# Three score products and neighbouring value products of the sample group written to different partition groups of PSUM

## The reference, cut to what matters

```
s_c = einsum('bqgrd,bcgd->bgrqc', qg, kc) + tab[...]        # 63 compressed keys
...
s_s = einsum('bqgrd,bgqksd->bgrqks', qg, k_sel) + tab[...]  # up to 16 blocks of 64 keys
...
s_w = einsum('bqgrd,bkgd->bgrqk', qg, kvw[:, :, 0]) + tab[...]   # 513 window keys
...
o_x = einsum(p_x, v_x)          # p_x = masked softmax(s_x), for each of the three branches
```

## Time and profile before

| | |
|---|---|
| median of 3 runs | 1839.0 us (1838.51 to 1839.18) |
| the profiled execution | 1834.96 us, span 1833.4 us, mean TensorE clock 0.907 of full |
| TensorE matmul busy | 1605.6 us, 88% |
| VectorE busy | 759.3 us, 41% |
| ScalarE busy | 504.2 us, 28% |
| GpSimd busy | 108.2 us, 6% |
| sample group | about 1400 to 1750 us of the span |

### The profile page before, as it was taken

How to read it: one execution, slowest core, us unless ns; L and a number is a source line. 1 busy time by engine, 2 the same in 40 slices (tenths; PEclk the granted TensorE clock), 3 DMA queues, 4 the chain that set the end, 5 groups by cost and what they waited for, 6 DMA issues and landing times. The chain is left out here.

```text
span 1833.4 us, 22894 instructions
## 1 busy us (share of the span) xinstructions
PE 1605.6 (88%) x8053; PEld 1234.2 (67%) x8053; DVE 759.3 (41%) x1821; ACT 504.2 (28%) x919; POOL 108.2 (6%) x147
## 2 busy tenths in 40 slices
PE   6989999998987998989999999996675888888686
PEld 3877787777765786878768767765353655566375
DVE  3057776776676102001541460451652333344313
ACT  3133233323331100021331332332441233333102
POOL 0011112111210000000010001001000000000000
PEclk7989999999997997998997997996786999999888
DMA  5075435543460340242052015004005544442111
GB/s 174 3 208 164 141 93 164 161 143 92 135 192 26 105 124 1 70 104 69 1 117 57 24 44 130 23 0 133 6 1 160 143 134 120 116 116 70 47 56 47
DMA packets 141544, 170.20 MB, mean 93 GB/s; under 512 B 46532, under 2 KB 108348, under 8 KB 141132
## 3 DMA queue, kind: packets, MB, share of 16 engines
q1 hardware_dynamic: 130120, 129.38, 24.4%
q0 software_dynamic: 11344, 39.79, 7.9%
HBM read 149.20 MB, written 24.32 MB: 95 GB/s over the span
## 5 line engine op out<-in xcount | busy, mean ns | idle before, releaser
L273 PE MATMUL psum<-arena 128*128 128x260 f32 x1536 | 356.2, 390 | 7.4 <-DMA arena<-in_ssd_w_in 7.4
L1484 PE MATMUL psum<-arena 128*128 128x260 f32 x1408 | 335.3, 396 | 7.8 <-DMA arena<-in_nsa_w_in 5.4
L273 PEld LDWEIGHTS psum<-arena 128*128 128x128 f32 x1536 | 291.8, 192 | 60.4 <-DMA arena<-in_ssd_w_in 7.8
L1484 PEld LDWEIGHTS psum<-arena 128*128 128x128 f32 x1408 | 271.2, 196 | 64.4 <-issue 12.5
L326 PE MATMUL psum<-arena 128*128 128x128 f32 (+9 forms) x1367 | 198.2, 289 | 96.5 <-DVE arena L1763 24.0
L326 PEld LDWEIGHTS psum<-arena 128*128 128x128 f32 (+9 forms) x1367 | 154.3, 148 | 148.3 <-issue 57.9
L1053 PE MATMUL psum<-arena 128*128 128x260 f32 x656 | 149.4, 390 | 8.8 <-PEq L593 6.9
L1053 PEld LDWEIGHTS psum<-arena 128*128 128x128 f32 x656 | 127.0, 194 | 31.0 <-issue 9.6
L1190 PE MATMUL psum<-arena 128*128 128x252 f32 x512 | 123.8, 404 | 5.4 <-ACT arena L1185 5.4
L1190 PEld LDWEIGHTS psum<-arena 128*128 128x128 f32 x512 | 103.7, 205 | 22.3 <-issue 4.8
L1688 ACT ACTIVATE arena<-arena 128x128 f32<-128x128 f32 (+3 forms) x128 | 71.9, 562 | 131.6 <-DVE arena L1780 126.8
(11 more groups left out here) (261 smaller groups left out, 1740.1 us busy)
## 6 DMA issues: line engine op xcount, KB each, us to landing
arena<-in_cache_kv SPq DMA_DIRECT2D x128, 256.0 KB, 4.1
arena<-in_ssd_w_in SPq DMA_DIRECT2D x16, 1024.0 KB, 5.4
arena<-in_nsa_w_in SPq DMA_DIRECT2D x16, 1024.0 KB, 5.2
arena<-scr_rows POOLq DMA_DIRECT2D x16, 520.0 KB
arena<-in_ssd_w_in SPq DMA_DIRECT2D x16, 512.0 KB
arena<-scr_rows POOLq DMA_DIRECT2D x8, 1024.0 KB, 6.5
arena<-in_state_ssm POOLq DMA_DIRECT2D x16, 512.0 KB, 6.9
out_ssm_sample<-arena POOLq DMA_DIRECT2D x16, 512.0 KB, 7.0
```

The lines of the kernel that those rows point to most:

```text
L273: mm = nc.tensor.matmul(psum[:, b + h, 0:HALF], w[:, k, n % 2 * P:(n % 2 + 1) * P], xn[:, k, h * HALF:(h + 1) * HALF], start=(k == 0), sto ...
L1484: mm = nc.tensor.matmul(psum[:, pair + h, 0:HALF], w[:, k, at * P:(at + 1) * P], xn[:, k, h * HALF:(h + 1) * HALF], start=(k == 0), stop=( ...
```

## The change

Three places. On TensorE the scores of the two key halves and of the window (now all on L1951, g outside, the three key sets inside) go to PSUM partitions 0, 32 and 64; the value products of neighbouring key tiles go in turn to partitions 0 and 32 (`out(r, n % 2)`), the compressed branch's product moves behind the eight selected ones. On VectorE the bias addition of the selected scores is split by halves, since they lie in different partitions, and the two halves of the selected and of the window output are added while they are taken out of PSUM: two copies and two additions instead of two copies, with one more wait of VectorE for itself.

```
-                for a in range(2):
-                    for g in range(2):
-                        nc.tensor.matmul(psum[0:NH, a, :], qcur[:, g, :], kselt[:, g, a, :], start=(g == 0), stop=(g == 1))
+                keys = (lambda g: kselt[:, g, 0, :], lambda g: kselt[:, g, 1, :],
+                        lambda g: kwint[:, g].rearrange("p a n -> p (a n)"))
                 for g in range(2):
-                    nc.tensor.matmul(psum[0:NH, 2, :], qcur[:, g, :], kwint[:, g].rearrange("p a n -> p (a n)"),
-                                     start=(g == 0), stop=(g == 1))
+                    for a in range(3):
+                        nc.tensor.matmul(psum[32 * a:32 * a + NH, a, :], qcur[:, g, :], keys[a](g),
+                                         start=(g == 0), stop=(g == 1))
...
-                def out(r):
-                    return psum[0:NH, 2, r * 256:(r + 1) * 256] if r < 2 else psum[0:NH, 0, 0:256]
+                def out(r, e):
+                    return psum[32 * e:32 * e + NH, 2, r * 256:(r + 1) * 256] if r < 2 else psum[32 * e:32 * e + NH, 0, 0:256]
...
-                nc.tensor.matmul(out(0), pcT[0:NCS, NH:2 * NH], vcmp[0:NCS, :], start=True, stop=True)
                 for n in range(8):
-                    nc.tensor.matmul(out(1), ptb[:, n * NH:(n + 1) * NH], pages_s[j][:, n % 4, n // 4, 256:512],
-                                     start=(n == 0), stop=False)
-                nc.tensor.matmul(out(1), ptn[:, 0:NH], vnew[j][:, 0:256], start=False, stop=True)
+                    nc.tensor.matmul(out(1, n % 2), ptb[:, n * NH:(n + 1) * NH], pages_s[j][:, n % 4, n // 4, 256:512],
+                                     start=(n < 2), stop=(n == 6))
+                nc.tensor.matmul(out(0, 0), pcT[0:NCS, NH:2 * NH], vcmp[0:NCS, :], start=True, stop=True)
+                nc.tensor.matmul(out(1, 1), ptn[:, 0:NH], vnew[j][:, 0:256], start=False, stop=True)
                 for n in range(4):
-                    nc.tensor.matmul(out(2), ptb[:, (8 + n) * NH:(9 + n) * NH], wins[j][:, n % 2, n // 2, 256:512],
-                                     start=(n == 0), stop=False)
-                mm = nc.tensor.matmul(out(2), ptn[:, NH:2 * NH], vnew[j][:, 256:512], start=False, stop=True)
+                    nc.tensor.matmul(out(2, n % 2), ptb[:, (8 + n) * NH:(9 + n) * NH], wins[j][:, n % 2, n // 2, 256:512],
+                                     start=(n < 2), stop=(n == 3))
+                mm = nc.tensor.matmul(out(2, 0), ptn[:, NH:2 * NH], vnew[j][:, 256:512], start=False, stop=True)
...
-                nc.vector.tensor_tensor(row[:, S_WIN:S_NEWW], psum[0:NH, 2, :], bias[:, S_WIN:S_NEWW], ALU.add)
-                s.link(nc.vector.tensor_tensor(row[:, S_SEL:S_NEWS].rearrange("p (a n) -> p a n", a=2), psum[0:NH, 0:2, :],
-                                               bias[:, S_SEL:S_NEWS].rearrange("p (a n) -> p a n", a=2), ALU.add), score_used)
+                nc.vector.tensor_tensor(row[:, S_WIN:S_NEWW], psum[64:64 + NH, 2, :], bias[:, S_WIN:S_NEWW], ALU.add)
+                nc.vector.tensor_tensor(row[:, S_SEL:S_SEL + NPAIR], psum[0:NH, 0, :], bias[:, S_SEL:S_SEL + NPAIR], ALU.add)
+                s.link(nc.vector.tensor_tensor(row[:, S_SEL + NPAIR:S_NEWS], psum[32:32 + NH, 1, :],
+                                               bias[:, S_SEL + NPAIR:S_NEWS], ALU.add), score_used)
...
                 nc.vector.tensor_copy(o_head[0:NH, 0:512], psum[0:NH, 2, :])
-                s.link(nc.vector.tensor_copy(o_head[0:NH, 512:768], psum[0:NH, 0, 0:256]), os_out)
+                s.link(nc.vector.tensor_copy(o_head[0:NH, 512:768], psum[32:32 + NH, 0, 0:256]))
+                nc.vector.tensor_tensor(o_head[0:NH, 256:512], o_head[0:NH, 256:512], psum[32:32 + NH, 2, 256:512], ALU.add)
+                s.link(nc.vector.tensor_tensor(o_head[0:NH, 512:768], o_head[0:NH, 512:768], psum[0:NH, 0, 0:256], ALU.add),
+                       os_out)
```

More of the change, by code:

```diff
@@ L1840, in _build @@
     dve_smp = sig("dve_smp", 0)
-    dve_smp.per = 15
+    dve_smp.per = 16
     dve_end = sig("dve_end", 5)
```

## The result

The changed kernel takes 1793.81 us in the median of 4 runs (1792.48 to 1795.87), the kernel before 1838.76 (1837.17 to 1839.18): a ratio of 0.9761, 95% interval [0.9734, 0.9788]. The profiled execution took 1793.02 us with a span of 1791.5, 41.9 us less than the span before. The forecast was 1795 us with a range of 1785 to 1810.

What follows compares the result with a forecast made beforehand. TensorE was taken as the bound in the sample group's turns. Terms -23.7 - 23.4 + 2.1 + 0.6 + 0.8 = -43.6 us, against the 1839.0 us median, gave 1795.4, rounded to 1795 us; range 1785 to 1810.

Steps and rivals of the forecast that it cites:

- scores, seven turns: TensorE's score matmuls: three column groups overlap, 5.31 to 1.93 us, saving 3.38 us in each of seven turns, 23.7 us.
- value products, eight turns: TensorE's value products: eight matmuls deep in two groups, 6.74 to 3.81 us, saving 2.93 us a turn, 23.4 us.
- hand-over: From value products to next scores: VectorE's additions delay os_out, so scores start 0.3 us later, seven times, +2.1 us.
- bias additions: VectorE's split bias addition before the reordering copies TensorE awaits: 1.20 to 1.27 us, eight times, +0.6 us.
- end of the stage: After turn 7, outputs go to TensorE's L2036 with nothing beside them, so the output additions cost +0.8 us.
- clock: TensorE's granted clock: no net change taken, between -15 and +24 us; the rival, more half-clock time, +14 to +21, chance 0.12.
- Turn 0: First turn of the sample group: score saving lost, as TensorE idles some 3 us for L1173, which waits for pages.
- some 47 us: Expected fall of TensorE's busy time in the changed profile.
- the two additions bring about 0.77 us: VectorE's output additions, each costing what a copy does, make os_out 0.77 us later.
- Page loads: Rival: page loads become the bound; 3 us late in six turns gives 1813 us; chance 0.03.
- slower rival: TensorE's 16-row products don't overlap and each group change drains the array, 0.09 us each: 1857 us; chance 0.04.
- blocked rival: A matmul's two records block each other on TensorE: scores 3.2 us, about 1812 us, scores alone 1804; chance 0.10.

Runs made afterwards that it cites:

- e7 to e10: Changed kernel with reordering copies moved earlier (1787.39 us); that with four partition groups (1773.88); four groups, TensorE gap filled with extra matmuls (1776.58); changed kernel, gap filled (1782.91).

## Why the prediction was right, and where by luck

The path was right: both products shortened as forecast, and the additions were paid where the forecast said. The total was right to 1 us, which is less than the errors of its terms, and that is luck: three small costs came out 5.1 us higher together, the clock gave 2.6 back, and the medians fell by 45.0 us where the profiled executions, from which the terms are read, fell by 41.9. Against the profiled executions:

| term | forecast | measured |
|---|---|---|
| scores, seven turns | -23.7 | -23.8 (5.31 to 1.91 us; not in turn 0) |
| value products, eight turns | -23.4 | -23.6 (7 x 2.89, and 3.33 in turn 7) |
| hand-over | +2.1 | +3.7 (1.64 to 2.17 us, seven times) |
| bias additions | +0.6 | +2.8 (0.35 a turn) |
| end of the stage | +0.8 | +2.1 (1.1 before L2036, 1.0 behind it) |
| clock | 0 | -2.6 in turns 1 to 6 |

The terms measured sum to -41.4, the span fell by 41.9; 0.3 of the rest is an earlier start of the stage.

- **The scores and the value products** were costed from the nearest rows, the scores from L1563 (four records deep), the value products from 0.217 us a record of their own group (eight matmuls deep), and both durations came out within 0.04 us. Three groups cost no more than two. By the 2.38 times of the Trainium skill, "TensorE: Matmul & The Clock Gate" (Part 3, the measured speedups), they would have taken 2.23 us; the trace has 5.31 / 1.91 = 2.78 times, so the row was the better guide.
- **Turn 0** lost its score saving as said: L326 starts at 1409.01, before at 1409.83, of which 0.3 us are an earlier start of the stage. The busy time of TensorE does fall there, which the forecast of "some 47 us" left out: it fell by 53.8.
- **The hand-over** was named rightly: VectorE's L2177 is now what the scores wait for. The step that failed is "the two additions bring about 0.77 us": it took the overlap of neighbouring instructions for granted, which is lost when they read different partitions. L2174 to the end of L2177 are 1.98 us, not 1.77, and the delay behind it came to 0.53, not 0.3. Without the change of partitions (VectorE's part alone) they are 1.79 and 0.33 us, as forecast.
- **The bias additions** failed for the same reason. The step "1.20 us becomes twice 0.67 less the overlap" gave 0.07. From the start of L2120 to that of the maximum behind them are 2.88 us now and were 2.53, which is 0.35; without the change of partitions it is 0.06.
- **The end of the stage**: from L2174's start to L2036's are 8.36 us now (1695.50 to 1703.86) and were 7.27, the additions again (1.1). The other 1.0 us stands behind L2036, in blocks that the change doesn't touch: from there to the end are 86.6 us before and 87.6 after. It is not the additions, since the kernel without any (no additions, one group a branch) has 87.5; the kept traces range from 86.0 to 87.7.
- **The clock** was forecast as no change, and was near it in sum, but not in its parts. Turns 1 to 6 took 36.1 to 40.1 us; before, turn 1 took 41.6 and turns 2 to 6 took 44.2 to 44.7. If turns 1 to 6 were all at full clock, they would take 6 x 36.1 = 216.7 us; they take 228.1, so 11.4 us are lost to the clock; before 263.4 against 6 x 41.56 were 14.0. The forecast's reason for a zero, a loss in turn 0 against gains elsewhere, has its sign right: the time at half clock went from 3.4 to 6.8 us in turn 0 and from 34 to 27 us in turns 1 to 6. The two halves alone show that the sign could as well have been another: with the value products alone nothing is lost in these turns, with the scores alone each turn has a stretch.
- **Page loads**: "I see no sign of it" was too sure. SyncE's waits were counted, but not the time from a load's issue to its first use. The changed kernel just touches it (1.0 us once); in e7 to e10, with turns of 34 to 36 us, it costs 3.3 to 7.0 us.
- **The drains** of the slower rival don't exist between groups; only the change from 128 to 63 rows and back has its 0.1 us (L2002 to L2003 are 0.53 us for two records).
- **The blocked rival** was wrong for this change, but blocking of another kind exists: in the order that keeps a group together it showed from the fifth record of a group on.

## What to carry to other kernels

Float32 products with 16 output rows took 0.36 of their time with their outputs in three groups of 32 PSUM partitions and 0.57 in two; what is left is the depth of the deepest group, and, by the one layout that was tried, another group should come up after at most four records of one in the order of the matmuls. Then read what the shorter products expose: here VectorE's order of work, the clock and a slow series of load issues each held back some 7 to 15 us, and a filled or removed gap in front of dense matmuls was worth more (12 to 15 us filled, 7 removed) than the next microsecond a turn saved in the products (3 us, within the noise). Sums over turns should be made at one clock first, and the clock's share stated apart, since a version that saves 1.2 us of work in each turn can gain nothing that stands clear of the noise. And a matmul and its weight load can report the same wait, so their rows in a list of waits are not to be added.

## What the runs showed of the hardware that was not expected

- With eight records of one partition group in front, a record of an idle group started only with the fifth of them; with four in front it started at once (groups not alternating: 5.15 us instead of 3.84, scores unchanged at 1.92). That the queue takes four records of a group ahead is inferred from this.
- Neighbouring VectorE instructions on different partition starts begin 0.70 us apart where those on the same begin 0.60 apart (16 x 512 float32), so 0.1 us a change: the second starts when the first has ended, and no longer 0.07 us before.
- Adding some 1.7 us of needless matmuls to each of seven turns made the kernel 12 to 15 us faster: in turns 1 to 6 TensorE was granted 2.4 GHz where it had 1.2 for 41 us (four groups) and for 24 of 27 us (the change).
- The granted clock was 1.00 through all of turns 1 to 6 with the value products alone changed, which leaves 5.3 us of 16-row scores in each turn, while with the scores alone changed there was a stretch at 1.2 GHz in every turn. Why the one keeps it and the other not stays open.
